# Filler matmuls around the turns and first products of the index stage, and beside the narrow matmuls of the recurrence, in a two-layer decode kernel

## The reference, cut to what matters

```
# the recurrence, by chunks, its state carried on:
o = einsum(qc * exp(b), S) + einsum(att, vc)
S = exp(bl)[..., None] * S + einsum(kc * exp(bl - b), vc)
# the scores of the index stage (8 heads of width 64):
isc = relu(einsum('bthd,bsd->bths', iqb, ik_all))
isc = einsum('bths,bth->bts', isc, iwb)
top, sel = top_k(where(k_pos <= q_pos, isc, -inf), topk)
```

## Time and profile before

| | before |
|---|---|
| median of 3 runs | 2033.56 us |
| runs | 2032.27 to 2034.12 us |
| the profiled execution's own time | 2037.58 us |
| its span, first to last instruction | 2035.9 us |
| PE busy | 2000.2 us (98%) |
| PEld busy | 1781.0 us (87%) |
| DVE busy | 1250.6 us (61%) |
| ACT busy | 728.6 us (36%) |
| mean granted TensorE clock | 0.996 |
| chain that ended last | PE 92%, DVE 4%, ACT 2%, issue 1% |

### The profile page before, as it was taken

One profiled execution on the slowest core, in us unless ns is written; L12 is line 12 of the kernel. 1 busy time (PEld: TensorE's weight loads), 2 busy tenths in 40 slices (PEclk: granted clock), 3 DMA queues, 4 the chain that ended last, 5 costly groups with the idle time before them and its releaser, 6 DMA issues.

```text
span 2035.9 us, 35440 instructions
## 1 busy us (share of the span) xinstructions
PE 2000.2 (98%) x14254; PEld 1781.0 (87%) x14254; DVE 1250.6 (61%) x2107; ACT 728.6 (36%) x1141; POOL 289.5 (14%) x275
## 2 busy tenths in 40 slices
PE   9999999999999999999999999999999999999998
PEld 7767898889989999999998587679989999999998
DVE  5478478776354677437745799774454667625753
ACT  5344435523323333213334426453332333212323
POOL 1022004432001000000003356421000200000000
PEclk9999999999999999999999999999999999999999
DMA  6478223523642222222224325733453222222222
GB/s 219 148 269 308 90 83 105 183 82 114 232 166 78 79 83 84 83 83 84 80 79 134 104 83 182 236 104 115 156 185 131 77 85 85 95 84 83 86 68 77
DMA packets 221589, 249.53 MB, mean 123 GB/s; under 512 B 18562, under 2 KB 175500, under 8 KB 221222
## 3 DMA queue, kind: packets, MB, share of 16 engines
q1 hardware_dynamic: 200614, 200.27, 30.5%
q0 software_dynamic: 9872, 28.65, 4.2%
q10 hardware_dynamic: 10940, 18.35, 2.7%
HBM read 234.15 MB, written 13.00 MB: 121 GB/s over the span
## 4 chain that ended last, share of the span: by engine, by line
PE 92%; DVE 4%; ACT 2%; issue 1%; PEld 1%; DMA 0%; PEldq 0%; ACTq 0%; POOL 0%; DVEq 0%
PE PS L984 25%; PE PS L1022 19%; PE PS L1027 10%; PE PS L962 10%; PE PS L1096 6%; PE PS L1029 5%; PE PS L1519 1%; PE PS L1537 1%; PE PS L1765 1%; PE PS L1911 1%; PE PS L1548 1%; DVE stat L3029 1%; PE PS L1193 1%; PE PS L1560 1%; PE PS L1218 1%
## 5 line engine op out<-in xcount | busy, mean ns | idle before, releaser
L2843 DVE TENSOR_TENSOR W_r<-W,WH 128x1024 fp32r<-128x1024 f32 (+1 forms) x219 | 287.2, 1334 | 300.6 <-ACT WH L2062 300.3
L2062 ACT ACTIVATE WH<-W 128x1024 fp32r<-128x1024 f32 (+1 forms) x262 | 266.5, 1034 | 415.1 <-PE PS L984 148.6
L1022 PE MATMUL PS<-hx_r,WH 128*128 128x320 f32 x1280 | 308.0, 310 | 0.0
L984 PE MATMUL PS<-hx_r,WH 128*128 128x256 f32 (+1 forms) x1216 | 255.0, 299 | 0.0
L984 PE MATMUL PS<-arena_r,WH 128*128 128x256 f32 (+1 forms) x912 | 233.5, 297 | 0.0
L1027 PE MATMUL PS<-hx_r,WH 128*128 128x512 f32 x640 | 233.0, 398 | 0.0
L1022 PEld LDWEIGHTS PS<-hx_r,WH 128*128 128x128 f32 x1280 | 220.7, 188 | 6.9
L984 PEld LDWEIGHTS PS<-hx_r,WH 128*128 128x128 f32 x1216 | 199.6, 190 | 0.7 <-issue 0.7
L1022 PE MATMUL PS<-hx_r,W_r 128*128 128x320 f32 x640 | 198.1, 309 | 0.0
L984 PE MATMUL PS<-hx_r,W_r 128*128 128x320 f32 (+1 forms) x640 | 190.1, 297 | 0.0
L1029 PE MATMUL PS<-hx_r,W_r 128*128 128x256 f32 x640 | 180.0, 281 | 0.0
(11 more groups left out here) (509 smaller groups left out, 3959.7 us busy)
## 6 DMA issues: line engine op xcount, KB each, us to landing
W<-in_w_ffn_in SPq DMA_DIRECT2D x176, 256.0 KB, 3.3
W<-in_w_ffn_out SPq DMA_DIRECT2D x40, 512.0 KB, 3.4
W<-in_w_in_ab SPq DMA_DIRECT2D x28, 512.0 KB, 3.7
C<-in_cache_mem_k SPq DMA_DIRECT2D x10, 1024.0 KB, 9.7
C<-in_cache_diff_k POOLq DMA_DIRECT2D x32, 256.0 KB, 4.7
C<-in_cache_diff_k SPq DMA_DIRECT2D x32, 256.0 KB, 3.8
W<-in_w_xk SPq DMA_DIRECT2D x16, 512.0 KB, 3.3
W<-in_w_xv SPq DMA_DIRECT2D x16, 512.0 KB, 3.6
```

Source lines behind the costliest of these rows:

```text
L984: ins = mm(o, w[:, k, c * 128:c * 128 + 128], v(k0 + k)[:, t0:t1], start=opens and first and k == 0 and e == 0, stop=last and k == nk - 1 ...
L1022: ins = mm(early, w[:, k, cols], v(k0 + k)[:, 0:EARLY], start=first and k == 0 and e == 0, stop=last and k == nk - 1 and e == 2, skip_grou ...
L2062: fn(slot_view(WH, NV, n), slot_view(W, NW, n), ACT.Copy).then_inc(hi_done, 1)
L2843: v_.tensor_tensor(slot_view(WL, NW, n), slot_view(W, NW, n), plain(slot_view(WH, NV, n)), ALU.subtract).then_inc(lo_done, 1)
```

## The change

`keep_warm` takes an output region and an operand. Fillers of 128 columns are issued in these places, 40 in all: 3 ahead of each of the two groups of `L1401` (into the bank that the group has opened); 8 ahead of `L1420` (into unused columns of the bank that it fills); in the index stage, into unused columns of bank 4: 4 after the turn of tile 2, 4 after the turn of tile 3, 2 after the heads' weights, and 2 after each of the 8 heads of `prompt_index(1)`. Bank 4 belongs to the projection before, so the two waits for its readers (`proj_act`, `proj_dve`) move up, from behind the heads' weights to behind the turn of tile 2.

```
-            def keep_warm(count):
-                warm = misc[:, 0:64].bitcast(bf16)
+            def keep_warm(count, out=tbank(4)[:, 0:128], warm=misc[:, 0:64].bitcast(bf16)):
                 for _ in range(count):
-                    mm(tbank(4)[:, 0:128], warm, warm, start=True, stop=True)
+                    mm(out, warm, warm, start=True, stop=True, skip_group_check=True)
...
                 t = open_tr("A")
+                keep_warm(3, t[:, 0:128], identb[:, :])
                 for b in range(4 * g, 4 * g + 4):
...
+            keep_warm(8, bank(own_bank)[:, 256:384], identb[:, :])
             for b in range(NB):
                 mm(all_own[:, :, 8 * b:8 * b + 8], L["s0q"][:, b, :], heads_of[:, :, 8 * (b % 4):8 * (b % 4) + 8],
                    start=b == 0, stop=False, skip_group_check=True)
...
+            beside_sums = tbank(4)[:, 256:384]
...
             for i in range(1, 4):
                 pe.wait_ge(handoff["iq_rot"], i // 2 + 1)
                 tr_unit("A", [(e * 128, L["i_tm"][:, i, 128 * e:128 * e + 128]) for e in range(4)])
+                if i == 2:
+                    pe.wait_ge(proj_act, pj.count("A", len(pj.who)))
+                    pe.wait_ge(proj_dve, pj.count("D", len(pj.who)))
+                    keep_warm(4, beside_sums, identb[:, :])
+            keep_warm(4, beside_sums, identb[:, :])
...
             mm(t[:, 0:64], const("heads", 8), L["iwT"][0:8, :], start=True, stop=True).then_inc(tr_done, 1)
-            pe.wait_ge(proj_act, pj.count("A", len(pj.who)))
-            pe.wait_ge(proj_dve, pj.count("D", len(pj.who)))
+            keep_warm(2, beside_sums, identb[:, :])
...
-            prompt_index(1, range(8))
+            for h in range(8):
+                prompt_index(1, [h])
+                keep_warm(2, beside_sums, identb[:, :])
```

## The result

The changed kernel takes 2038.44 us, the median of 9 runs (2035.15 to 2041.71). The kernel before, on the same chip, takes 2033.56 us (9 runs, 2031.55 to 2036.2). The ratio is 1.0020 with a 95% interval of 1.0012 to 1.0029: slower, by 4.1 us (2.4 to 5.9); the medians lie 4.9 us apart. I had forecast 2034.7 us, in a range of 2030.5 to 2036.2.

A forecast was written before the change was run, and what follows sets the result against it. PE was taken to bound the kernel, busy 98% of the span and 92% of the chain. Profiled 2037.58 - 4.4 (clock) + 1.35 (fillers) gave 2034.5, median 2033.56 + 1.35 gave 2034.9; forecast 2034.7 us, range 2030.5 to 2036.2.

The forecast's parts named there:

- 2 behind each of seven heads: Index stage, prompt_index(1): two fillers per head, 0.11 us, fit into 0.17 us of slack while DVE paces; without cover 0.8 us.
- The rival that I gave 0.05: In prompt_index(1) fillers take the heads' slack and PE becomes the pace; slower, 2038.3 us; chance 0.05.
- the 1.35 that I had for them: Whole kernel: forecast cost in us of the 24 or so fillers on the path, 0.34 + 0.45 + 0.45 + 0.11.
- Recurrence 0.79 forecast: Recurrence: fillers cost 0.34 us ahead of the L1401 groups and 0.45 us ahead of L1420, without gaps on PE.
- Turns 0.45: Index stage: 4 + 4 fillers among the turns delay DVE's read-out and the second head's bank by 0.45 us.
- the 0.78 us that I called lost in the L1435 group: Recurrence: eight L1435 records took 1.70 us at the low clock where 0.92 was expected at 2.4 GHz.
- not 1.77: Recurrence: low clock's forecast cost in us, 0.78 in the L1435 records plus 0.99 in the block behind them.
- not 2.6: Index stage: low clock's forecast cost in us, 1.82 in sample_index and 0.8 for PE's last head.
- not 4.4: Both touched stages: us to win back if the clock holds, 1.77 recurrence and 2.6 index stage; bounds 3.6 and 5.1.
- Most runs without a profile have neither fall: Unprofiled runs: clock falls in neither stage, so fillers only cost there: 2033.56 + 1.35 = 2034.9 us.
- the two roads: Two ways to the forecast: profiled execution less falls plus fillers, 2034.5 us; median run plus fillers, 2034.9 us.
- That rival had 0.15: Fillers don't hold the clock where it would fall, as in the recurrence's 32-column records; 2034.9 or 2035.2 us; chance 0.15.

The follow-up runs named there:

- e3: The changed kernel without the 16 fillers between the heads of prompt_index(1), the other 24 kept; 2035.62 us, ratio 1.0010 to the kernel before.
- e4: The kernel before with only the 16 fillers between the heads and the moved waits; 2039.07 us, ratio 1.0023.
- e6: The changed kernel with the heads' fillers on 64 rows, on the same half as the head ahead; 2035.34 us, ratio 1.0004 to the kernel before.
- e12: One more traced execution of e4 (only the fillers between the heads, and the moved waits); 2038.31 us.
- e1: The kernel before run again unchanged, with each run's mean granted clock; 2034.62 us, ratio 1.0005.
- e8: The kernel before with only the 10 fillers among the turns and behind the heads' weights; 2034.05 us, ratio 1.0002.
- e5: The changed kernel with the heads' fillers in four groups of 4, one behind each second head; 2036.56 us, ratio 1.0012 to the kernel before.
- e9: The changed kernel with 1 filler and not 2 behind each head of prompt_index(1); 2040.33 us, ratio 1.0026 to the kernel before.
- e11: The changed kernel unchanged, one more execution with its trace; 2039.08 us.

## Why the prediction was wrong

- **The step that failed** is "2 behind each of seven heads: 0.11 us each into 0.55 - 0.38 = 0.17 us of slack per head. Hidden as long as DVE paces". The 0.38 us a head came from three heads that overlapped on different halves of the rows. A full-height filler between them ends the overlap: 0.63 us for a head by itself, 0.22 for the two fillers, 0.85 in all. So the slack of 0.17 was a lack of 0.30, and the eight heads take 6.77 us against 4.25 in e3: 2.5 us that I had at 0.11. e4 shows the place and e6 the mechanism.
- **The rival that I gave 0.05** (the fillers take the heads' slack, PE becomes the pace) was the right one for the place. It named 0.17 us per pair as the point of decision and a switch of number formats as the cause. The pair's price with the lost overlap is 0.85 - 0.38 = 0.47 us. The switch of formats isn't it, since e6's fillers are bf16 too and cost 0.11 us in all. Its time, 2038.3 us, is next to the measured 2038.44 by luck: it had 1.0 us for the heads, which took 2.5, and 2.4 more for the other 24 fillers, which cost less than the 1.35 that I had for them.
- **The other prices.** Recurrence 0.79 forecast, and 0.61 delays the kernel. Two misses cancel there: the fillers beside L1401 take 0.67 and not 0.34 (the same change of mode fits, since its weights have 32 columns, but wasn't tested), and I took the stretch to be without a wait, while PE waits for DVE ahead of the second block (e12). Turns 0.45, measured 0.44. The moved waits show no cost. The sum at the high clock is 0.61 + 0.44 + 2.52 = 3.6 us against 1.35; runs at 0.999 say 3.3, and the ratio 4.1, with 3.6 inside its interval.
- **What the low clock costs.** In the changed kernel the L1435 group takes 0.91 us from its first record to the block (1.09 by the chain; I had 0.92), the block 6.40, sample_index 2.00, as forecast. But the 0.78 us that I called lost in the L1435 group wasn't lost: from its first record to the block it is 1.48 us in the kernel before, with the fall (421.20 to 422.68), and 1.48 in e12 without it, where PE waits for DVE. From L1401 to the end of the second block the kernel before took 24.07 us (406.29 to 430.36) and e12 23.02, so the fall cost 1.05 (1.2 in e1) and not 1.77. In the index stage it was 2.4 and not 2.6: 1.82 of sample_index and 0.6 of the heads, where I had 0.8. Together some 3.5 us could come back, not 4.4.
- **"Most runs without a profile have neither fall"** doesn't hold. By their clocks 75 of 94 runs of the kernel before are under 0.999, and both of its traces have both falls. The 4.0 us between the profiled execution and the median are no measure of two falls; that execution was among the lowest by clock. This moved the forecast little, since the two roads met; that they met was luck, as the 4.4 was too high.
- **Do the fillers hold the clock?** In the recurrence no: it fell in three of eight traces with them (e5, e9, e11) and in three of six without (the two of the kernel before, e8). That rival had 0.15. In the index stage the ones among the turns may: it fell in one of eight traces with them (e9, at 1120.6) and in three of six without (the two of the kernel before, e12). That is too few to show it. What they can save there, 1.82 + 0.6 = 2.4 us in the executions that fall, is no more than what the heads' fillers cost in every one.

What stays open: how often the clock falls in each stretch. Fourteen traces of ten versions are too few for a rate, and nothing here shows why it falls in one execution and not in the next. Open too is why the start differs by 2 us.

## What to carry to other kernels

Before putting anything between two small matmuls, ask whether they overlap: a per-item time that is far under the time of one alone (0.38 against 0.63 us) says so. Here a filler of the same height, on the rows of the matmul ahead of it, kept the overlap, and one of full height ended it. Put fillers where the chain shows PE waiting for another engine, not where a busy share looks low. A wait that the chain before doesn't show can still be there: with the clock low, PE seemed to have no wait in the recurrence, and at the high clock it waited for DVE. And look at the mean clock and at the start of the first changed instruction before reading a difference of a few us from two profiles; here the slower kernel had the shorter profiled span.

## What the runs showed of the hardware

- Between the 64-row heads, two full-height bf16 matmuls of 128 columns cost 0.47 us a head, one costs 0.41 (0.79 - 0.38), and two of 64 rows 0.11 us over seven heads: DVE's pace of 0.53 us held.
- The kernel before on one chip had mean clocks from 0.996 to 0.999 and times from 2031.26 to 2038.27 us; over all 94 runs it is about 1.5 us for each 0.001. The clock fell in the same two stretches in some executions and not in others, with one kernel too: in the recurrence in e11 and in neither of the other two traces of the changed kernel, among the heads in e12 and not in e4.
- Near the start the granted clock of a window can read 1.00 while PE works at the pace of the low level: three 128-column bf16 matmuls in 0.52 us in e4 and in 0.33 in e12.
- PE was not idle for long in or ahead of any of the falls (0.38 us in the earlier trace rows): in e12 PE counts as busy through all of the window from 1120 to 1121 us (1.00) while the clock stays at 0.50 for 10.2 us.
